# A decoder trunk on one core: the fourth weight sum of the gate/up strips formed by an adding transfer

## The chip, the core and the metric

The kernel runs on one core of a Trainium2 chip. The core has a matrix engine (TensorE, PE in the profile; PEld is its weight load), VectorE (DVE), ScalarE (ACT), GpSimd (POOL) and SyncE (SP), and 16 DMA engines that move data between the chip's main memory and the core's SBUF. The engines run side by side, each in the order of its own instructions, and wait for each other by semaphores. The metric is device time in microseconds of one execution, lower is better. Times of before are one profiled execution and three timed runs.

## The reference, cut to what matters

Two residual layers over 256 tokens of width 2048, all in float32. Each layer has a mixer, a cross attention into 256 memory tokens, and a SwiGLU feed-forward part:

```python
D_FF = -(-8 * D_MODEL // (3 * 256)) * 256     # 5632

def swiglu(h, w_gate, w_up, w_down):
    return (jax.nn.silu(h @ w_gate) * (h @ w_up)) @ w_down

for layer in range(DEPTH):                    # 2
    x = x + rmsnorm(mix, g[1])                # stick-breaking + pooling, or gated linear attention
    x = x + rmsnorm(memory_cross_attention(...), g[3])
    h = rmsnorm(x, g[4])
    x = x + rmsnorm(swiglu(h, ffn_w_gate[layer], ffn_w_up[layer], ffn_w_down[layer]), g[5])
```

The change touches `h @ w_gate` and `h @ w_up` alone: 256 x 2048 times 2048 x 5632, twice per layer.

## The kernel before

**Precision by splitting.** A float32 weight block w is split into a rounded part `w_hi`, written by ScalarE (`hi`, L542), and the rest `w_lo = w - w_hi`, written by VectorE (`lo`, L1017). The activations are split the same way. One product is then three matmuls: hi by hi, lo by hi, hi by lo.

**Strips and chunks.** Weights come in chunks of 128 x 2048 floats (1 MB, 8 KB on each of 128 partitions). SyncE loads them into five slots `wide0` to `wide4`, in turn (`load`, L330). ScalarE and VectorE split each chunk into one of four slots of `w_hi` and `w_lo`. A strip is 512 columns of each of two matrices (here gate and up) and takes eight chunks, n to n+7.

**Seven products in place of eight.** In most strips the first four chunks are treated as a 2 x 2 block matrix of weights b11, b12, b22, b21 (`B11, B12, B22, B21 = 0, 1, 2, 3` in order of loading), and the product is formed with seven block products in place of eight, from sums of weight blocks and sums of token blocks (`s_hi`, `s_lo`). So such a strip splits eleven chunks (`SUMMED = 11`), c to c+10: c = b11; c+1 = b11 + b12 (in `w_sum`); c+2 = the third sum (in b11's slot); c+3 = b21 as loaded; c+4 = the second sum (in b12's slot); c+5 = b22; c+6 = the fourth sum (in b21's slot); c+7 to c+10 = the last four chunks, n+4 to n+7, as they are. VectorE forms the four sums (`add`, L1021): three in `lead`, and the fourth at the head of `rest11`:

```python
dve.wait_ge(add_done, 4 * g + 3)
add(b21, b11, b21)
```

**What sets the order.** Each engine's program is written out by hand. On VectorE a strip is: split of c, three sums, splits of c+1 and c+2, the elementwise work of the strip before (`gather`: L1085 and L1522), split of c+3, the fourth sum, splits of c+4 to c+10. On ScalarE the copies of c to c+10 in the same order, with some moves between PSUM banks between them (L592 behind c+3; L600 behind c+4; L605 and L606 behind c+5, L614 behind c+7), of which TensorE waits for L614 ahead of product c+6. On TensorE one product per chunk c to c+6 (12 matmuls each; each waits for that chunk's `w_lo`), two per chunk c+7 to c+10, eight transposes behind c+3. A copy of chunk j waits until product j-4 is done (`w_used`), since there are four slots.

**When a slot is loaded again.** `slot_free` lists, load by load, the count that SyncE waits for: b11's slot is free when the fourth sum is done (it is its last reader), b12's when c+4 is split, b22's when c+5 is, b21's when c+6 is, and the last four when c+7 to c+10 are. With five slots, b11's slot takes the strip's sixth chunk, n+5, which is c+8. SyncE issues strictly in order.

**Where.** Per layer the gate/up stage has 11 strips, the first with eight plain products and ten with block sums, 20 in all. In other stages 15 more strips have block sums. In the gate/up stage GpSimd has nothing to do but to spill `xres` to memory ahead of it, to load a row of gains, and to reload `xres` once the tenth strip's product c+5 is done (`reload_x`, L434). GpSimd's transfers have a queue of their own.

Of the kernel before, what the change touches and what calls it, by code (L numbers as in the profile page):

```python
# [19 lines left out]
WIDE = 5  # L20
# [1 line left out]
SUMMED = 11  # L22
B11, B12, B22, B21 = 0, 1, 2, 3

Strip = namedtuple("Strip", "c n g a u")


def build(nc, x, mem, norms, mem_norm, even_w_in, pool_w, pool_scale, even_w_out, odd_w_in, gate_w,
# [14 lines left out]


    plan = {}
    at = {"c": 0, "n": 0, "g": 0, "a": 0, "u": 0, "r": 0, "rf": 0}
    slot_free = []
    STRIPS = FF // NB

    def stage(name, seven=(), rounds=0, rows=0, taken=True):  # L50

        pl = plan[name] = dict(at, strips=[])
        for summed in seven:
            st = Strip(at["c"], at["n"], at["g"] if summed else None, at["a"], at["u"])
            pl["strips"].append(st)
            for k in range(8):
                if summed and k == B11:  # L60
                    slot_free.append((1, 4 * st.g + 4))
                else:
                    chunk = {B12: 4, B22: 5, B21: 6}.get(k, k + 3) if summed else k
                    slot_free.append((0, 2 * (st.c + chunk + 1)))
            at["c"] += SUMMED if summed else 8
            at["n"] += 8
            at["g"] += 1 if summed else 0
            at["a"] += 2
            at["u"] += 1
        for k in range(rows):  # L70
            slot_free.append((0, 2 * (at["c"] + k + 1)))
        at["c"] += rows
        at["n"] += rows
        at["a"] += 1 if rows else 0
        at["u"] += 1 if rows else 0
        at["r"] += (rounds if taken else 0) + (1 if rows else 0)
        at["rf"] += rounds
# [6 lines left out]
    for l in range(LAYERS):  # L84
        stage(f"pre_mix{l}", rounds=2)
        if l == 0:
            stage("sb_qk", (False, True), rounds=2)
            stage("sb_z", rounds=1)
            stage("sb_vu", (True, True))
            stage("sb_sum", rounds=1)  # L90
            stage("sb_pv", rounds=1)
            stage("pool_mean", rounds=1)
            stage("pool_map", rounds=1)
        else:
            stage("gla_qk", (False, True), rounds=2)
            stage("gla_a", rounds=1)
            stage("gla_at", rounds=1)
            stage("gla_g", rounds=1)
            stage("gla_v", (False, True))
            stage("gla_s", rounds=1)  # L100
            stage("gla_r", (True, False))
            stage("gla_o", rounds=GH // 2)
            stage("gla_t", rounds=2)
        stage(f"mix_out{l}", (False, False))
        stage(f"pre_x{l}", rounds=2)
        stage(f"xq{l}", (False, True), rounds=2)
        stage(f"x_s{l}", rounds=1)
        stage(f"x_pt{l}", rounds=1)
        stage(f"x_pv{l}", rounds=2)
        stage(f"x_out{l}", (False, False))  # L110
        stage(f"pre_ff{l}", rounds=2)
        stage(f"gu{l}", (False,) + (True,) * (STRIPS - 1), rounds=STRIPS, taken=False)
        stage(f"down{l}", rows=FT)
    NORMS = ["mem_norm"] + [f"{n}{l}" for l in range(LAYERS) for n in ("pre_mix", "pre_x", "pre_ff")]
    POSTS = [f"{n}{l}" for l in range(LAYERS) for n in ("mix_out", "x_out", "down")]
# [6 lines left out]
    def sums_used(name, i):  # L122

        return strip_of(name, i).c + 6 + W_SLOTS
# [5 lines left out]
    with ExitStack() as ctx:  # L130
# [13 lines left out]
        def sem(name):  # L144
            return ctx.enter_context(nc.semaphore(name))
# [85 lines left out]

        wide_full = [sem(f"wide_full{i}") for i in range(WIDE)]
        add_done = sem("add_done")
        snap = sem("snap")
        prod_done = sem("prod_done")
        mid_taken = sem("mid_taken")
# [83 lines left out]
        @block.sync  # L320
        def _(sp):
            def load(n, src):

                if n >= WIDE:
                    summed, count = slot_free[n - WIDE]
                    sp.wait_ge(add_done if summed else lo_done, count)
                dst = wide[n % WIDE][:]
                if len(src.shape) == 3:
                    dst = dst.rearrange("p (k n) -> p k n", k=4)
                sp.dma_start(dst, src).then_inc(wide_full[n % WIDE], 16)  # L330

            def strip(st, w0, col0, w1, col1):

                order = [(q, s) for q in range(2) for s in range(4)]
                if st.g is not None:
                    order = [(0, 0), (1, 0), (1, 1), (0, 1), (0, 2), (0, 3), (1, 2), (1, 3)]
                for k, (q, s) in enumerate(order):
                    w, col = ((w0, col0), (w1, col1))[q]
                    load(st.n + k, cut(w, s)[:, :, col:col + NB])

            def strips(name, w, col0=0):
                for i, st in enumerate(plan[name]["strips"]):
                    col = col0 + i * 2 * NB
                    strip(st, w, col, w, col + NB)

            for l in range(LAYERS):
                strips(f"mk{l}", wk[l])
                strips(f"mv{l}", wv[l])
            for l in range(LAYERS):
                if l == 0:  # L350
                    strips("sb_qk", even_w_in)
                    strips("sb_vu", even_w_in, 2 * SBW)
                    strips("mix_out0", even_w_out)
                else:
                    strips("gla_qk", odd_w_in)
                    strips("gla_v", odd_w_in, 2 * GH * GK)
                    strips("gla_r", odd_w_in, 2 * GH * GK + GH * GV)
                    strips("mix_out1", odd_w_out)
                strips(f"xq{l}", wq[l])
                strips(f"x_out{l}", wo[l])  # L360
                for i, st in enumerate(plan[f"gu{l}"]["strips"]):
                    strip(st, w_gate[l], i * NB, w_up[l], i * NB)
                for k in range(FT):
                    load(plan[f"down{l}"]["n"] + k, w_down[l][k * P:(k + 1) * P, :])

            for m in range(MT):
                sp.wait_ge(x_done, 2 * len(POSTS) - 1 + m)
                sp.dma_start(out[m * P:(m + 1) * P, :], xres[:, m, :]).then_inc(y_out, 16)
            sp.wait_ge(y_out, 16 * MT)
# [3 lines left out]
        def _(pool):  # L373
            then = stepper(pool, pool_step)

            def load_gain(row):
                pool.dma_start(gain[:], row.partition_broadcast(P)).then_inc(gain_in, 16)
# [93 lines left out]
            for l in range(LAYERS):  # L471
# [37 lines left out]
                spill_x(2 * (3 * l + 2))  # L509
                pool.wait_ge(y_scaled, y_banks)  # L510
                load_gain(norms[l, 5])
                reload_x(2 * l + 1, sums_used(f"gu{l}", STRIPS - 1))
                if l < LAYERS - 1:
                    pool.wait_ge(work_full[7], plan[f"gu{l}"]["rf"] + STRIPS)
# [13 lines left out]
        def _(act):  # L528
# [30 lines left out]
            def lead(st, before_1=nothing, before_3=nothing):  # L559

                if st.g is None:
                    split(st, 0)
                    before_1()
                    split(st, 1)
                    split(st, 2)
                    before_3()
                    split(st, 3)
                    return
                hi(st.c, landed(st.n + B11))
                before_1()  # L570
                act.wait_ge(add_done, 4 * st.g + 1)
                hi(st.c + 1, w_sum[:, (st.c + 1) % W_SLOTS, :])
                act.wait_ge(add_done, 4 * st.g + 3)
                hi(st.c + 2, wide[(st.n + B11) % WIDE][:])
                before_3()
                hi(st.c + 3, landed(st.n + B21))
# [9 lines left out]
            def rest11(st, q_sb, p5_sb, reuse=(), before_5=nothing, before_9=nothing):  # L586
# [3 lines left out]
                act.wait_ge(w_used, c + 1 + W_SLOTS)  # L590
                act.wait_ge(bank_free[1], st.u + 1)
                nc.scalar.activation(ps[:, 1, :], ps[:, 0, :], ACT.Copy, scale=-1.0).then_inc(snap, 1)  # L592
                act.wait_ge(add_done, 4 * g + 2)
                hi(c + 4, wide[(st.n + B12) % WIDE][:])

                before_5()
# [7 lines left out]
                act.wait_ge(bank_free[3], st.u + 1)  # L604
                nc.scalar.activation(ps[:, 3, :], ps[:, 1, :], ACT.Copy).then_inc(snap, 1)  # L605
                nc.scalar.activation(q_sb, ps[:, 1, :], ACT.Copy).then_inc(snap, 1)  # L606
                act.wait_ge(add_done, 4 * g + 4)
                hi(c + 6, wide[(st.n + B21) % WIDE][:])
                split_wide = lambda j: hi(c + j, landed(st.n + j - 3))
                split_wide(7)  # L610
# [384 lines left out]
        def _(dve):  # L995
# [32 lines left out]
            def lead(st, before_1=nothing, before_3=nothing):  # L1028
# [15 lines left out]
                dve.wait_ge(w_used, c + 2)  # L1044
                add(w_sum[:, (c + 1) % W_SLOTS, :], b11, b12)
                loaded(st.n + B22)
                dve.wait_ge(add_done, 4 * g + 1)
                add(b12, b22, b12)
                dve.wait_ge(add_done, 4 * g + 2)
                add(b11, b12, b11)  # L1050
                lo(c + 1, w_sum[:, (c + 1) % W_SLOTS, :])
                lo(c + 2, b11)
# [11 lines left out]
            def rest11(st, before_5=nothing, before_7=nothing):  # L1064
                c, g = st.c, st.g
                b11, b12, b22, b21 = (src_of(st.n + k) for k in range(4))
                dve.wait_ge(add_done, 4 * g + 3)
                add(b21, b11, b21)
                lo(c + 4, b12)
                before_5()  # L1070
                lo(c + 5, b22)
                lo(c + 6, b21)
                before_7()
                for j in range(7, SUMMED):
                    lo(c + j, src_of(st.n + j - 3))
# [942 lines left out]
```

## Time and profile before

| | |
|---|---|
| median of 3 runs | 3009.91 us (2999.89, 3009.91, 3010.01) |
| the profiled execution | 2999.51 us, span of its instructions 2997.8 us |
| TensorE busy | 2886.9 us (96%) |
| VectorE busy | 2069.6 us (69%), of which 240.4 are 105 sums into `wide` |
| ScalarE busy | 1534.2 us (51%) |
| GpSimd busy | 99.6 us (3%) |
| moved by DMA | 583.44 MB, 195 GB/s over the span |
| mean granted TensorE clock | 0.985 |

The span is the time from the first to the last instruction of the execution that the profiler recorded. An engine is busy while one of its instructions runs; waiting and issuing transfers are not counted. A share over the whole span mixes stages with different limits, so what an edit in one stage is worth is read from that stage.

### The profile page before, as it was taken

Reading aid. Unit: us, or ns where it says so; the run is one execution under the profiler, and the core shown is the slowest. Engines: PE = TensorE matmul, PEld = TensorE weight load, DVE = VectorE, ACT = ScalarE, POOL = GpSimd, SP = SyncE. Lnnn points to the kernel's source line nnn. Section 1 sums busy time; section 2 is a strip of 40 time slices with the busy share of each in tenths; the row PEclk is TensorE's granted clock in tenths of the full one; section 3 lists DMA queues with packets and bytes.
Section 4 is the critical chain, followed back from the end, with each engine's and each line's share of the span. In section 5 each row is a group of like instructions: output and inputs, shape, how many; then the busy total and the mean of one; then the engine's idle time right before and its main releaser. Section 6 shows DMA issues by size and latency. Waiting matters only on the chain. (4 is left out here: it accounts for less than half of the span.)

```text
span 2997.8 us, 31678 instructions
## 1 busy us (share of the span) xinstructions
PE 2886.9 (96%) x13082; PEld 2389.9 (80%) x13082; DVE 2069.6 (69%) x1359; ACT 1534.2 (51%) x1363; POOL 99.6 (3%) x112
## 2 busy tenths in 40 slices
PE   7999999999999999999998999999999999999998
PEld 5888788778777888887887877777787788887887
DVE  6888778448348888885555758546646888886454
ACT  4666556445345556664344545444534665565443
POOL 0000000010010000000002000001001000000000
PEclk9999999999999999999999989999999999999999
DMA  7665744644445556556554615653554655565552
GB/s 266 225 255 180 282 179 157 242 166 173 166 165 204 183 202 225 216 182 252 193 195 157 213 68 187 238 204 133 197 182 168 219 182 182 204 225 226 205 189 96
DMA packets 237984, 583.44 MB, mean 195 GB/s; under 512 B 8720, under 2 KB 8736, under 8 KB 222096
## 3 DMA queue, kind: packets, MB, share of 16 engines
q1 hardware_dynamic: 232608, 530.61, 49.7%
q0 software_dynamic: 4064, 38.21, 3.2%
q10 hardware_dynamic: 1168, 12.59, 1.0%
q8 instruction: 104, 1.70, 0.2%
q14 instruction: 40, 0.33, 0.0%
HBM read 564.60 MB, written 16.78 MB: 194 GB/s over the span
## 5 line engine op out<-in xcount | busy, mean ns | idle before, releaser
L1017 DVE TENSOR_TENSOR w_lo<-wide,w_hi 128x2048 fp32r<-128x2048 f32 x550 | 1250.4, 2289 | 540.2 <-ACT w_hi L542 538.4
L542 ACT ACTIVATE w_hi<-wide 128x2048 fp32r<-128x2048 f32 x550 | 1048.8, 1914 | 557.1 <-PE ps L1568 443.4
L1568 PE MATMUL ps<-w_hi,act_hi 128*128 128x512 f32 x3332 | 1222.4, 393 | 36.2 <-DVE act_lo L1159 22.2
L1568 PE MATMUL ps<-w_hi,act_lo 128*128 128x512 f32 x3332 | 1217.3, 391 | 0.0
L1568 PE MATMUL ps<-w_lo,act_hi 128*128 128x512 f32 x3332 | 1217.1, 391 | 0.0
L1568 PEld LDWEIGHTS ps<-w_hi,act_hi 128*128 128x128 f32 x3332 | 629.6, 189 | 172.3 <-issue 30.8
L1568 PEld LDWEIGHTS ps<-w_hi,act_lo 128*128 128x128 f32 x3332 | 629.3, 189 | 131.7
L1568 PEld LDWEIGHTS ps<-w_lo,act_hi 128*128 128x128 f32 x3332 | 630.0, 189 | 130.7 <-issue 0.2
L1021 DVE TENSOR_TENSOR wide<-wide,wide 128x2048 f32<-128x2048 f32 x105 | 240.4, 2290 | 5.0
L1568 PE MATMUL ps<-w_hi,s_hi_x 128*128 128x512 f32 x528 | 211.1, 400 | 14.5 <-DVE nat L1513 6.3
L1568 PE MATMUL ps<-w_hi,s_lo_x 128*128 128x512 f32 x528 | 207.9, 394 | 0.0
L1568 PE MATMUL ps<-w_lo,s_hi_x 128*128 128x512 f32 x528 | 207.7, 393 | 0.0
L975 ACT ACTIVATE act_hi<-mid 128x256 fp32r<-128x256 f32 x80 | 33.4, 418 | 240.6 <-PE ps L1568 240.6
L1568 PEld LDWEIGHTS ps<-w_hi,s_hi_x 128*128 128x128 f32 x528 | 100.5, 190 | 36.1 <-DVE nat L1513 7.1
L1568 PEld LDWEIGHTS ps<-w_hi,s_lo_x 128*128 128x128 f32 x528 | 100.5, 190 | 21.5
L1568 PEld LDWEIGHTS ps<-w_lo,s_hi_x 128*128 128x128 f32 x528 | 100.7, 191 | 20.3
L1538 DVE TENSOR_TENSOR act_lo<-mid,act_hi 128x256 fp32r<-128x256 f32 x88 | 36.9, 424 | 114.1 <-ACT act_hi L975 114.1
L542 ACT ACTIVATE w_hi<-w_sum 128x2048 fp32r<-128x2048 f32 x35 | 67.2, 1921 | 88.1 <-DVE w_sum L1021 58.2
L1021 DVE TENSOR_TENSOR w_sum<-wide,wide 128x2048 f32<-128x2048 f32 x35 | 80.1, 2290 | 29.2 <-PE ps L1568 29.2
L718 ACT ACTIVATE ps<-ps 128x512 f32<-128x512 f32 x48 | 27.9, 582 | 117.9 <-DVE y L1209 117.9
L1017 DVE TENSOR_TENSOR w_lo<-w_sum,w_hi 128x2048 fp32r<-128x2048 f32 x35 | 79.9, 2284 | 0.0
L1209 DVE TENSOR_TENSOR y<-ps,gain 128x512 f32<-128x512 f32 x48 | 31.9, 687 | 66.1 <-PE ps L1568 42.7
(212 smaller groups left out, 1393.8 us busy)
## 6 DMA issues: line engine op xcount, KB each, us to landing
wide<-in_ffn_w_gate SPq DMA_DIRECT2D x88, 1024.0 KB, 7.6
wide<-in_ffn_w_up SPq DMA_DIRECT2D x88, 1024.0 KB, 7.2
wide<-in_ffn_w_down SPq DMA_DIRECT2D x88, 1024.0 KB, 4.9
wide<-in_odd_w_in SPq DMA_DIRECT2D x48, 1024.0 KB, 5.3
wide<-in_xattn_wk SPq DMA_DIRECT2D x32, 1024.0 KB, 8.3
wide<-in_xattn_wv SPq DMA_DIRECT2D x32, 1024.0 KB, 6.8
wide<-in_even_w_in SPq DMA_DIRECT2D x32, 1024.0 KB, 7.1
wide<-in_xattn_wq SPq DMA_DIRECT2D x32, 1024.0 KB, 5.1
```

The costliest lines, as they stand in the source:

```text
L542: nc.scalar.activation(w_hi[:, c % W_SLOTS, :], src, ACT.Copy).then_inc(hi_done, 2)
L718: nc.scalar.activation(bank, bank, ACT.Square, accum_out=ssq_part[:, m, part:part + 1])\
L975: nc.scalar.activation(act_hi[:, s % 4, :], mid[:, s, :], ACT.Copy).then_inc(jit_hi, 1)
L1017: nc.vector.tensor_tensor(w_lo[:, c % W_SLOTS, :], src, w_hi[:, c % W_SLOTS, :].bitcast(F32), ALU.subtract).then_inc(lo_done, 2)
L1021: nc.vector.tensor_tensor(out, a, b, ALU.add).then_inc(add_done, 1)
L1209: nc.vector.tensor_tensor(y[:, m, cols], ps[:, b, :], gain[:, cols], ALU.mult).then_inc(y_scaled, 1)
L1538: nc.vector.tensor_tensor(act_lo[:, s % 4, :], mid[:, s, :], act_hi[:, s % 4, :].bitcast(F32), ALU.subtract).then_inc(jit_done, 1)
L1568: return nc.tensor.matmul(dst, lhs, rhs, start=start, stop=stop, skip_group_check=loose)
```

## The change

The fourth sum is no longer a VectorE instruction in the 20 gate/up strips. GpSimd issues a transfer in its place, whose source is b11's slot and whose destination is b21's slot, with an adding operation: what is in the destination is read, the source added, and the sum written back. The 15 strips of other stages keep the VectorE instruction. A strip now also carries `k`, its first count of `add_done` (three sums per strip with the transfer, four else), and `d`, its number among the transfers (None without one). GpSimd waits for the third sum and for the split of c+3, the last reader of the loaded b21. ScalarE's copy of c+6 waits for the transfer (`dma_sum`, 16 per transfer), and so does SyncE before it loads into b11's slot.

```diff
-                    slot_free.append((1, 4 * st.g + 4))
+                    slot_free.append((2, 16 * (st.d + 1)) if by_dma else (1, st.k + 4))
...
+            at["k"] += (3 if by_dma else 4) if summed else 0
+            at["d"] += 1 if summed and by_dma else 0
...
-        stage(f"gu{l}", (False,) + (True,) * (STRIPS - 1), rounds=STRIPS, taken=False)
+        stage(f"gu{l}", (False,) + (True,) * (STRIPS - 1), rounds=STRIPS, taken=False, by_dma=True)
...
-                    sp.wait_ge(add_done if summed else lo_done, count)
+                    sp.wait_ge((lo_done, add_done, dma_sum)[summed], count)
...
                 pool.wait_ge(y_scaled, y_banks)
                 load_gain(norms[l, 5])
+                for i in range(1, STRIPS):
+                    st = strip_of(f"gu{l}", i)
+                    b11, b21 = (wide[(st.n + k) % WIDE] for k in (B11, B21))
+                    pool.wait_ge(add_done, st.k + 3)
+                    pool.wait_ge(lo_done, 2 * (st.c + 4))
+                    pool.dma_start(b21[:], b11[:], accum_op=ALU.add).then_inc(dma_sum, 16)
                 reload_x(2 * l + 1, sums_used(f"gu{l}", STRIPS - 1))
...
-                act.wait_ge(add_done, 4 * g + 4)
+                if st.d is None:
+                    act.wait_ge(add_done, st.k + 4)
+                else:
+                    act.wait_ge(dma_sum, 16 * (st.d + 1))
                 hi(c + 6, wide[(st.n + B21) % WIDE][:])
...
-                dve.wait_ge(add_done, 4 * g + 3)
-                add(b21, b11, b21)
+                if st.d is None:
+                    dve.wait_ge(add_done, st.k + 3)
+                    add(b21, b11, b21)
                 lo(c + 4, b12)
```

The other waits on `add_done` change from `4 * g` to `st.k` as their base, and nothing else.

On VectorE, before, from the split of c+3 to that of c+7 in the gate/up strip whose b21 lies in slot `wide0` (b11 in `wide2`):

```order
L1017 TENSOR_TENSOR w_lo_56<-wide0_49,w_hi_54 128x2048
L1021 TENSOR_TENSOR wide0_49<-wide2_51,wide0_49 128x2048
L1017 TENSOR_TENSOR w_lo_56<-wide3_52,w_hi_54 128x2048
L1017 TENSOR_TENSOR w_lo_56<-wide4_53,w_hi_54 128x2048
L1017 TENSOR_TENSOR w_lo_56<-wide0_49,w_hi_54 128x2048
L1017 TENSOR_TENSOR w_lo_56<-wide1_50,w_hi_54 128x2048
```

The second row goes, and the splits of c+4 and later follow the split of c+3 at once. On GpSimd, after, the transfers of the first layer stand between the row of gains and the reload of `xres`; each waits on two semaphores (here the last eight of the ten):

```order
L521 DMA wide1_50<-wide3_52 128x2048 [waits lo_done,add_done]
L521 DMA wide4_53<-wide1_50 128x2048 [waits lo_done,add_done]
L521 DMA wide2_51<-wide4_53 128x2048 [waits lo_done,add_done]
L521 DMA wide0_49<-wide2_51 128x2048 [waits lo_done,add_done]
L521 DMA wide3_52<-wide0_49 128x2048 [waits lo_done,add_done]
L521 DMA wide1_50<-wide3_52 128x2048 [waits lo_done,add_done]
L521 DMA wide4_53<-wide1_50 128x2048 [waits lo_done,add_done]
L521 DMA wide2_51<-wide4_53 128x2048 [waits lo_done,add_done]
L438 DMA xres_57<-x_scratch 128x4096 [waits w_used,x_kept]
```

Before, the reload of `xres` followed the row of gains directly; ten transfers now stand ahead of it.

## Rows read from the trace of the kernel before

**Rows 1.** The page: span, and busy time of each engine; weight loads (line group).
```profile
span 2997.8 us, 31678 instructions
PE 2886.9 (96%) x13082; PEld 2389.9 (80%) x13082; DVE 2069.6 (69%) x1359; ACT 1534.2 (51%) x1363; POOL 99.6 (3%) x112
...
L1568 PEld LDWEIGHTS ps<-w_hi,act_hi 128*128 128x128 f32 x3332 | 629.6, 189 | 172.3 <-issue 30.8
```

**Rows 2.** Busy time by stretch, both layers' ten gate/up strips with sums.
```profile
core 0: us, PE busy (x) PEld busy (x) DVE busy (x) ACT busy (x) POOL busy (x), PEclk, DMA share, GB/s
...
942.00:1359.00 417.00, 413.86 (x1866) 343.17 (x1865) 361.65 (x193) 254.44 (x193) 0.54 (x1) 1.00 0.56 203
...
2315.00:2732.00 417.00, 413.86 (x1859) 343.02 (x1858) 361.20 (x193) 254.31 (x192) 0.54 (x1) 1.00 0.55 202
```

**Rows 3.** Waits of TensorE, 908 to 1365 us: total, times, longest.
```profile
PE ps L1568 <- DVE nat L1513: 3.1, 1, 3.1
```

**Rows 4.** Timeline of VectorE: start us, us, instruction, [idle before <-releaser].
```profile
1192.03 2.29 DVE L1021 TENSOR_TENSOR w_sum<-wide,wide 128x2048 f32<-128x2048 f32 x1 [1.15 <-PE ps L1568]
...
1205.76 2.29 DVE L1017 TENSOR_TENSOR w_lo<-wide,w_hi 128x2048 fp32r<-128x2048 f32 x1
1207.97 2.28 DVE L1021 TENSOR_TENSOR wide<-wide,wide 128x2048 f32<-128x2048 f32 x1
1210.17 8.89 DVE L1017 TENSOR_TENSOR w_lo<-wide,w_hi 128x2048 fp32r<-128x2048 f32 x4
...
1230.28 2.29 DVE L1017 TENSOR_TENSOR w_lo<-wide,w_hi 128x2048 fp32r<-128x2048 f32 x1 [3.15 <-ACT w_hi L542]
1233.72 2.29 DVE L1021 TENSOR_TENSOR w_sum<-wide,wide 128x2048 f32<-128x2048 f32 x1 [1.15 <-PE ps L1568]
```

**Rows 5.** Timeline of ScalarE in the same strip.
```profile
1194.40 1.92 ACT L542 ACTIVATE w_hi<-w_sum 128x2048 fp32r<-128x2048 f32 x1 [1.88 <-DVE w_sum L1021]
...
1211.94 3.75 ACT L542 ACTIVATE w_hi<-wide 128x2048 fp32r<-128x2048 f32 x2
1217.30 0.58 ACT L614 ACTIVATE ps<-ps 128x512 f32<-128x512 f32 x1 [1.61 <-PE ps L1568]
...
1228.26 1.92 ACT L542 ACTIVATE w_hi<-wide 128x2048 fp32r<-128x2048 f32 x1 [3.52 <-PE ps L1568]
```

**Rows 6.** Timeline of TensorE where product c+6 of that strip starts.
```profile
1219.60 0.39 PE L1568 MATMUL ps<-w_hi,s_lo_x 128*128 128x512 f32 x1
1219.82 0.39 PE L1568 MATMUL ps<-w_hi,act_hi 128*128 128x512 f32 x1
```

**Rows 7.** Timelines of VectorE (578.94) and GpSimd (580.12, 580.71).
```profile
578.94 0.88 DVE L1292 SCALAR_TENSOR_TENSOR act_lo<-ps,vec,act_hi 128x256 fp32r<-128x256 f32 x2 [0.85 <-ACT act_hi L767]
...
580.12 0.56 POOL L377 DMA_DIRECT2D gain<-in_norms  x1 [46.95 <-DVE act_lo L1292]
580.71 0.54 POOL L498 DMA_DIRECT2D kx<-kv_scratch  x1
```

**Rows 8.** DMA engines, 1192.03 to 1233.72 us, 40 slices: busy tenths, rate.
```profile
DMA  3000000000000000003899999999999999999999
GB/s 147 26 0 0 0 0 0 0 0 0 0 0 0 0 0 0 0 0 75 291 409 411 381 399 230 377 377 366 409 405 399 389 385 389 387 387 381 393 389 346
```

**Rows 9.** Timeline of SyncE's queue; landing times of `wide`, 1192 to 1234 us.
```profile
1210.28 0.37 SPq L330 DMA_DIRECT2D wide<-in_ffn_w_gate  x1
...
DMA to landing us min/median/max: 4.9/7.7/8.2
```

**Rows 10.** GpSimd's DMA issues by stretch (1383 to 1390; 579 to 605): count, KB, landing.
```profile
pre_gain<-in_norms POOLq DMA_DIRECT2D x1, 1024.0 KB, 5.1
...
kx<-kv_scratch POOLq DMA_DIRECT2D x1, 2048.0 KB, 9.5
gain<-in_norms POOLq DMA_DIRECT2D x1, 1024.0 KB, 4.9
```

**Rows 11.** The trace's list of DMA issues: SyncE from SBUF.
```profile
out<-xres SPq DMA_DIRECT2D x2, 1024.0 KB, 3.9
```

**Rows 12.** The same list: GpSimd's 2 MB transfers beside other traffic.
```profile
xres<-x_scratch POOLq DMA_DIRECT2D x3, 2048.0 KB, 12.5
```

More of the change, by code:

```diff
@@ L23 @@
 B11, B12, B22, B21 = 0, 1, 2, 3
-Strip = namedtuple("Strip", "c n g a u")
+Strip = namedtuple("Strip", "c n g k d a u")
 def build(nc, x, mem, norms, mem_norm, even_w_in, pool_w, pool_scale, even_w_out, odd_w_in, gate_w,
@@ L45, in build, with stage @@
     plan = {}
-    at = {"c": 0, "n": 0, "g": 0, "a": 0, "u": 0, "r": 0, "rf": 0}
+    at = {"c": 0, "n": 0, "g": 0, "k": 0, "d": 0, "a": 0, "u": 0, "r": 0, "rf": 0}
     slot_free = []
     STRIPS = FF // NB
-    def stage(name, seven=(), rounds=0, rows=0, taken=True):
+    def stage(name, seven=(), rounds=0, rows=0, taken=True, by_dma=False):
         pl = plan[name] = dict(at, strips=[])
         for summed in seven:
-            st = Strip(at["c"], at["n"], at["g"] if summed else None, at["a"], at["u"])
+            st = Strip(at["c"], at["n"], at["g"] if summed else None, at["k"], at["d"] if by_dma else None,
+                       at["a"], at["u"])
             pl["strips"].append(st)
@@ L233, in build @@
         add_done = sem("add_done")
+        dma_sum = sem("dma_sum")
         snap = sem("snap")
@@ L570, in lead @@
                 before_1()
-                act.wait_ge(add_done, 4 * st.g + 1)
+                act.wait_ge(add_done, st.k + 1)
                 hi(st.c + 1, w_sum[:, (st.c + 1) % W_SLOTS, :])
-                act.wait_ge(add_done, 4 * st.g + 3)
+                act.wait_ge(add_done, st.k + 3)
                 hi(st.c + 2, wide[(st.n + B11) % WIDE][:])
@@ L592, in rest11 @@
                 nc.scalar.activation(ps[:, 1, :], ps[:, 0, :], ACT.Copy, scale=-1.0).then_inc(snap, 1)
-                act.wait_ge(add_done, 4 * g + 2)
+                act.wait_ge(add_done, st.k + 2)
                 hi(c + 4, wide[(st.n + B12) % WIDE][:])
@@ L1046, in lead @@
                 loaded(st.n + B22)
-                dve.wait_ge(add_done, 4 * g + 1)
+                dve.wait_ge(add_done, st.k + 1)
                 add(b12, b22, b12)
-                dve.wait_ge(add_done, 4 * g + 2)
+                dve.wait_ge(add_done, st.k + 2)
                 add(b11, b12, b11)
```

## The prediction

> **What bounds the kernel now.** I read the page's busy lines first. TensorE is busy 2886.9 of 2997.8 us and VectorE 2069.6 [rows 1], but these are averages over all stages, and the edit touches only the gate/up strips with block sums. So next I took the table of busy time by stretch for the two places where ten such strips run in each layer: in 417.00 us TensorE is busy 413.86, VectorE 361.65 and 361.20, at a granted clock of 1.00 [rows 2]. VectorE has 55 us to spare there and TensorE 3.1. The list of waits of TensorE puts all 3.1 us on one event, `nat` of VectorE's L1513, which happens in the first of the ten [rows 3]. So the strips are bound by the matmuls themselves. One strip lasts 1233.72 - 1192.03 = 41.69 us from one `w_sum` instruction to the next [rows 4].
>
> From here on I follow one strip, the one whose `w_sum` starts at 1192.03, and number its eleven split weight chunks c to c+10. The fourth sum, b21 = b11 + b21, becomes chunk c+6. On VectorE the last piece before it is the split of c+3 (1205.76, 2.29 us, so it ends at 1208.05), then the sum itself (1207.97, 2.28 us), then four splits in a row from 1210.17 [rows 4]. On ScalarE the copies of c+6 and c+7 are the pair that starts at 1211.94 [rows 5], so they start 1.7 us after the sum was ready. TensorE starts product c+6, the first matmul on `act_hi` after those on `s_hi_x`, at 1219.82, without a pause [rows 6].
>
> **What goes.** Ten strips in two layers lose one VectorE instruction each: 20 x 2.28 us = 45.6 us of VectorE time. None of it is on the path: what it leaves on VectorE is idle time, since the next `w_sum` waits for a matmul (the 1.15 us pause ahead of it [rows 4]) and TensorE has no gap to close. What it could free at most is the one gap of 3.1 us per layer [rows 3], 6.2 us in all, and even that gap is opened by work that stands ahead of the removed instruction. I count the removal at 0.
>
> **What comes: a transfer with a deadline.** GpSimd waits for the third sum and for the split of c+3, issues the transfer, and the copy of c+6 on ScalarE waits for its landing. Behind that copy ScalarE holds the copy of c+7 and the snapshot L614, without which TensorE may not start c+6 either. How late may the copy start? Backwards from 1219.82 [rows 6]: 0.19 for the weight load [rows 1] and 0.10 for a handoff, 2.29 for VectorE's split, 0.10 between ScalarE's end and VectorE's start (1228.26 + 1.92 = 1230.18 to 1230.28 [rows 4, 5]), 1.92 for the copy: 1219.82 - 4.60 = 1215.22. The snapshot path gives about the same: two copies from the same start, 3.75 us for the pair, and 0.58 [rows 5], are 4.33. From the end of the split of c+3, at 1208.05, this leaves 7.17 us.
>
> Of these, GpSimd's reaction takes 0.30: the VectorE piece at 578.94 lasts 0.88, to 579.82, and the transfer that waits for it is issued at 580.12 [rows 7]. ScalarE's reaction takes 0.08 (1192.03 + 2.29 to 1194.40 [rows 4, 5]). So the transfer may take 7.17 - 0.38 = 6.79 us from issue to landing before it costs anything; each microsecond above costs 20 us of the kernel, because the split of c+3 hangs on the former strip's matmuls and so moves with them.
>
> **How long does an adding transfer take?** The trace has none, so I bound it. In its time slot the DMA engines are idle: between about 1194 and 1210 the row shows zeros [rows 8], and SyncE's next load is issued only at 1210.28 [rows 9], which the edit moves behind the transfer. Quiet conditions therefore.
> - Low end: GpSimd's plain 1 MB transfer in such quiet landed after 5.1 us [rows 10], SyncE's from SBUF after 3.9 [rows 11]. Then it is hidden with 1.7 us or more to spare: cost 0.
> - Nearest for a transfer that reads both slots, 2 MB, and writes one: GpSimd issued 1 MB at 580.12 and 2 MB at 580.71; they landed 4.9 and 9.5 us later [rows 7, 10], at 585.02 and 590.21. The second 2 MB took 5.19 us, 2.6 per MB. So 5.1 + 2.6 = 7.7 us.
> - High end: GpSimd's 2 MB transfers beside other traffic took 12.5 us at the median [rows 12].
>
> I take 7.8: the 7.7, and 0.1 for the additional descriptors of a second source (my estimate, no row shows it). The excess over 6.79 is 1.0 us per strip, 20 us in all. At the high end it is 5.7 x 20 = 114 us.
>
> A rule of the Trainium skill speaks against the change here. The page "Collectives: The Full Stack", section "The bandwidth ceiling: the fold count and why AG ≠ RS ≠ AR", says that a reduce in the DMA engines reads two sources per chunk and so runs at about half of a copy, the add itself being free. No transfer in this trace adds, so only the changed kernel can show it; by the rule the data part doubles, as in my middle case. The Trainium skill's page "DMA: Bandwidth & Descriptors", section "Anatomy of one DMA — SWDGE (gpsimd) path", fits 2.0 us plus bytes over 436 GB/s, from which I estimate 4.4 us for 1 MB and 6.8 for 2 MB. The trace has 5.1 for the first, 0.7 more, so the rows decide; by the Trainium skill's figure the doubled transfer would just fit, and the time would be that of the first rival.
>
> **What is behind the transfer.** GpSimd has nothing else in these strips; its reload of `xres` stands behind the tenth and was issued after the strip's product c+5 anyway. SyncE is the queue that matters: the load of c+8 goes into b11's slot and now waits for the transfer, and all later loads behind it in order. In before it was issued at 1210.28, now at about 1216.2, 5.9 us later. It has to land by the copy of c+8: from the transfer's landing TensorE needs 4.6 us to start c+6, then 36 matmuls of 0.227 (1219.60 to 1219.82 [rows 6]), 8.2 us, and 4.6 of these are the copy, split and handoffs: 8.2 us are left for a load. SyncE's loads in this strip took 4.9 us at the least, 7.7 at the median and 8.2 at the most, sharing the DMA engines with each other [rows 9]. It fits. The burst itself needs 8 MB at about 390 GB/s, some 22 us (busy from 1211 to past 1233 [rows 8]), and now would end near 1240. The next strip's third block is the sixth of the eight, two loads (5.4 us) before the end, about 1234.5; VectorE wants it 2.4 us after the next `w_sum`, at 1237.1. Covered, with about 2 us.
>
> **Rivals.**
> - Hidden: the transfer lands within 6.8 us. Nothing changes but VectorE's busy time: 2999.5 us on the profile's scale, 3010 on the median's. For it: 5.1 and 3.9 for plain ones, the quiet slot, and an SBUF source. Against: it moves twice the reads. This is also the way to the other side, not slower; as a real gain it is worth at most the 6.2 us above, 0.2%.
> - A slow adder: the inline add or the two reads of one memory run at a third of the plain rate or below, 10 to 13 us. Excess 3.2 to 6.2, 64 to 124 us: 3075 to 3130. For it: no row shows what adding costs. Against: plain 2 MB alone need only 7.7.
> - Loads too late: the burst, 5.9 us later, is slower than reckoned by over 2 us (rows stored 2 KB at a time), so that the third block arrives after VectorE wants it. VectorE's chain to c+3 starts late, and with it the transfer: each microsecond costs 20 us again. With 1 us it is 20 us on top, 3050. Against: even the longest landing time of the strip, 8.2 us [rows 9], is no more than what is left.
> - GpSimd writes the descriptors slowly while VectorE works (it reads two SBUF slots at the time): issue took 0.54 to 0.60 us in all rows [rows 7], none longer, so I leave this inside the slow adder.
>
> **Numbers.** Forecast (7 to 9.5 us, 4 to 55 us more): 0.42. Hidden: 0.28. Slow adder: 0.23. Late loads: 0.05. A gain of any measurable size: 0.02. The sum is made on the profiled execution: 2999.5 us for a span of 2997.8, plus 20 = 3019.5. That execution is 10.4 us below the median of the three runs, 3009.91, which fall on two levels (2999.89; 3009.91, 3010.01). I forecast against the median: 3030 us. A range of its own for this case is 3005 to 3065; with the neighbours 2999 to 3110, which leaves out the top of the slow adder, about 0.12. 0.5% (15 us) is about what can be told from no change. A quarter of the forecast's case, below 0.75 us per strip, falls inside it: same 0.28 + 0.10 = 0.38; slower 0.60; faster 0.02.
>
> **What would show it.** Right: the page of after has 20 adding transfers of 1 MB that take 7 to 9.5 us; TensorE waits some 20 times for about 1 us at product c+6, on VectorE's split or on the snapshot; strips 42.7 us apart; VectorE busy 45.6 us less; the copy of c+6 waits for a DMA. The removal was free if no other gap of TensorE changes. Wrong: transfers under 6.8 us with strips still 41.7 apart (hidden); over 9.5 (slow adder); TensorE waiting at c+8 or VectorE waiting for loads ahead of its second sum (late loads).

## The result, and the profile after

The changed kernel takes 3020.98 us at the median of 7 runs (3017.68 to 3026.0), the one before 3005.94 us on the same occasion (7 runs, 2999.89 to 3010.03). The ratio is 1.005, 95% interval 1.0036 to 1.0064: 15 us slower, a small loss that is clear of noise. The profiled execution after took 3020.89 us, right at its median, while that of before (2999.51) lies at the low end of its runs. So of the 21.4 us between the two spans some 6 are the luck of the execution of before, and I count only what the strips show.

The page of after: span, busy time, and GpSimd's queue (packets, MB, share of 16 engines).

```profile
span 3019.2 us, 31698 instructions
...
PE 2897.7 (96%) x13082; PEld 2392.7 (79%) x13082; DVE 2028.2 (67%) x1339; ACT 1536.4 (51%) x1363; POOL 116.8 (4%) x132
...
q0 software_dynamic: 6944, 59.18, 6.6%
```

VectorE has 20 instructions and 41 us of busy time less than in [rows 1], GpSimd 20 instructions more. The strips got longer. The next rows are the ten `w_sum` instructions of each layer (count; min, median, max of one in ns; first and last start), of before and then of after:

```profile
L1021 DVE TENSOR_TENSOR w_sum<-wide,wide x10: 2284/2292/2294, 942.9 to 1317.1; 128x2048 f32<-128x2048 f32 x10
...
L1021 DVE TENSOR_TENSOR w_sum<-wide,wide x10: 2285/2292/2293, 2315.3 to 2691.1; 128x2048 f32<-128x2048 f32 x10
```

```profile
L1034 DVE TENSOR_TENSOR w_sum<-wide,wide x10: 2284/2288/2295, 946.0 to 1331.2; 128x2048 f32<-128x2048 f32 x10
...
L1034 DVE TENSOR_TENSOR w_sum<-wide,wide x10: 2284/2289/2293, 2333.1 to 2712.2; 128x2048 f32<-128x2048 f32 x10
```

Nine strips took 374.2 and 375.8 us before, and 385.2 and 379.1 after: 11.0 and 3.3 more, 14.3 in all, close to the 15.0 between the medians.

**One ordinary strip, 2458.67 to 2501.01.** VectorE's timeline of after (start, us; idle before, releaser). It answers to [rows 4].

```profile
2416.64 2.29 DVE L1034 TENSOR_TENSOR w_sum<-wide,wide 128x2048 f32<-128x2048 f32 x1
...
2458.67 2.29 DVE L1034 TENSOR_TENSOR w_sum<-wide,wide 128x2048 f32<-128x2048 f32 x1 [0.78 <-PE ps L1582]
...
2472.40 4.57 DVE L1030 TENSOR_TENSOR w_lo<-wide,w_hi 128x2048 fp32r<-128x2048 f32 x2
2477.39 2.29 DVE L1030 TENSOR_TENSOR w_lo<-wide,w_hi 128x2048 fp32r<-128x2048 f32 x1 [0.42 <-ACT w_hi L552]
2484.25 4.49 DVE L1030 TENSOR_TENSOR w_lo<-wide,w_hi 128x2048 fp32r<-128x2048 f32 x2 [4.57 <-ACT w_hi L552]
...
2498.80 2.29 DVE L1030 TENSOR_TENSOR w_lo<-wide,w_hi 128x2048 fp32r<-128x2048 f32 x1 [0.42 <-ACT w_hi L552]
2501.01 2.28 DVE L1034 TENSOR_TENSOR w_sum<-wide,wide 128x2048 f32<-128x2048 f32 x1
```

The splits of c+3 and c+4 now run as a pair, and before c+6 VectorE stands idle for 4.57 us: the 2.28 us that were removed have become waiting. The same strip on GpSimd, ScalarE (the copy of c+6 is the first of the pair at 2482.23; L627 is the snapshot that was L614) and TensorE (the start of product c+6), which answer to [rows 5, 6]:

```profile
2475.23 0.84 POOL L521 DMA_DIRECT2D wide<-wide  x1 [41.19 <-DVE w_lo L1030]
```

```profile
2482.23 3.73 ACT L552 ACTIVATE w_hi<-wide 128x2048 fp32r<-128x2048 f32 x2 [3.53 <-issue]
2485.86 0.59 ACT L627 ACTIVATE ps<-ps 128x512 f32<-128x512 f32 x1
```

```profile
2486.27 0.39 PE L1582 MATMUL ps<-w_hi,s_lo_x 128*128 128x512 f32 x1
2486.69 0.47 PE L1582 MATMUL ps<-w_hi,act_hi 128*128 128x512 f32 x1
```

Counted from `w_sum`, the transfer is issued at 16.56, the copy of c+6 starts at 23.56 (19.91 before), and product c+6 at 28.02 (27.79 before). TensorE's two matmuls are 0.42 us apart where 0.23 is the pace, so it waits 0.2 us. The list of waits leaves out so short a one, but twenty strips add them up.

The transfers themselves (issue time min, median, max in ns; landing):

```profile
L521 POOL DMA_DIRECT2D wide<-wide x20: 842/854/897, 961.4 to 2728.8; - x20
...
DMA to landing us min/median/max: 6.9/6.9/9.2
```

**Two more things cost.** First, w_sum starts are 42.03 us apart and then 42.34: the strip ends late in every second case. In the rows of VectorE the split ahead of `w_sum` at 2501.01 runs straight into it, where [rows 4] has a pause of 1.15 us. That split waited for ScalarE, and ScalarE for the load of the next strip's first block b11 (first row). In the second layer, 2315 to 2745 us, it waited for loads 16 times (total, times, longest); in the kernel before it waited for none in these strips:

```profile
2496.78 1.92 ACT L552 ACTIVATE w_hi<-wide 128x2048 fp32r<-128x2048 f32 x1 [0.79 <-DMA wide<-in_ffn_w_gate]
```

```profile
ACT w_hi L552 <- DMA wide<-in_ffn_w_up: 9.3, 7, 2.2
ACT w_hi L552 <- DMA wide<-in_ffn_w_gate: 7.4, 9, 1.1
```

Second, one transfer took 9.2 us. TensorE's list of waits (900 to 1390 us) and its timeline there:

```profile
PE ps L1582 <- DVE w_lo L1030: 5.7, 5, 3.0
```

```profile
1230.35 0.47 PE L1582 MATMUL ps<-w_hi,act_hi 128*128 128x512 f32 x1 [2.98 <-DVE w_lo L1030]
```

In that stretch, 1216 to 1227 us, an instruction fetch of 16 KB (q8) lay among the transfer's packets (q0). The traces of after, of the kernel with one wait and of the one that adds b21 to itself have two such transfers each: the six landed after 7.6 to 9.2 us, all others of after and of one wait after 6.9 to 7.0. That the fetch is what delays them is read from this coincidence; no run takes it away. The table by stretch shows the granted clock (third column from the end) falling after the wait, from 1.00 to 0.59 in the next 4 us, towards the lower of the two levels, 1.2 GHz:

```profile
q0 software_dynamic: 144, 1.05, 47.5%
q1 hardware_dynamic: 8, 0.02, 0.9%
q8 instruction: 1, 0.02, 0.6%
...
wide<-wide POOLq DMA_DIRECT2D x1, 1024.0 KB, 9.2
```

```profile
1226.00:1230.00 4.00, 1.38 (x7) 0.80 (x5) 2.08 (x1) 4.00 (x3) 0.00 (x0) 1.00 0.72 230
1230.00:1234.00 4.00, 3.65 (x9) 2.89 (x10) 3.04 (x3) 2.74 (x3) 0.00 (x0) 0.59 1.05 399
1234.00:1240.00 6.00, 6.00 (x28) 4.95 (x27) 5.15 (x3) 3.90 (x3) 0.00 (x0) 0.99 1.05 387
```

That strip lasted 45.85 us (`w_sum` at 1200.10 and 1245.95), 4 us above the 41.7 of before, and is over a quarter of the loss in this execution. The others were not traced, so whether each has such a strip stays open.

### The profile page after: what moved, and what is told of

It is laid out like the page before. It is cut to its first block and busy times, and to the rows that moved or that the text cites. A ratio compares the mean times of both kernels' runs of the same rounds, so it can differ in the third digit from the quotient of the medians.

```text
span 3019.2 us, 31698 instructions
## 1 busy us (share of the span) xinstructions
PE 2897.7 (96%) x13082; PEld 2392.7 (79%) x13082; DVE 2028.2 (67%) x1339; ACT 1536.4 (51%) x1363; POOL 116.8 (4%) x132
## 5 line engine op out<-in xcount | busy, mean ns | idle before, releaser
L1582 PE MATMUL ps<-w_hi,act_hi 128*128 128x512 f32 x3332 | 1224.5, 393 | 45.2 <-DVE act_lo L1173 22.7
L1034 DVE TENSOR_TENSOR wide<-wide,wide 128x2048 f32<-128x2048 f32 x85 | 194.7, 2291 | 5.0
L1582 PEld LDWEIGHTS ps<-w_hi,s_lo_x 128*128 128x128 f32 x528 | 100.4, 190 | 21.4
L1223 DVE TENSOR_TENSOR y<-ps,gain 128x512 f32<-128x512 f32 x48 | 31.9, 687 | 66.0 <-PE ps L1582 42.7
```

The costliest lines, as they stand in the source:

```text
L1034: nc.vector.tensor_tensor(out, a, b, ALU.add).then_inc(add_done, 1)
L1223: nc.vector.tensor_tensor(y[:, m, cols], ps[:, b, :], gain[:, cols], ALU.mult).then_inc(y_scaled, 1)
L1582: return nc.tensor.matmul(dst, lhs, rhs, start=start, stop=stop, skip_group_check=loose)
```

## The experiments

Three theories were at stake. A: the strip pays what the sum lands too late for product c+6. B: it pays because the loads behind the transfer are late. C: the relief of VectorE is worth something and hides part of the price. The copy of c+6 is counted from `w_sum`, which in the kernels with late loads is itself late in some strips. The kernels without a sum, with the plain copy, with half each and with the earlier split shared one set of runs of before; the loads held to c+5 and to c+6 and the two halves a second; the other three a third.

| kernel | ratio to before (95% interval) | landing, us | copy of c+6 after w_sum |
|---|---|---|---|
| after | 1.0050 (1.0036 to 1.0064) | 6.9 | 23.6 |
| no sum at all | 0.9999 (0.999 to 1.0008) | - | 19.9 |
| plain copy | 0.9999 (0.999 to 1.0008) | 4.5 | 21.1 |
| half each | 0.9999 (0.999 to 1.0008) | 4.5 | 21.2 |
| split of c+3 earlier | 1.0006 (0.9998 to 1.0015) | 6.9 | 22.7 |
| load held to c+5 (22.7) | 0.9998 (0.9989 to 1.0007) | - | 19.9 |
| load held to 23.7 | 1.0000 (0.9991 to 1.0009) | - | 19.9, in every second strip 19.1 |
| load held to c+6 (24.8) | 1.0080 (1.0067 to 1.0094) | - | 18.8 |
| two half transfers | 1.0028 (1.0017 to 1.0039) | 4.6, first half | 21.2, first half |
| adding b21 to itself | 1.0065 (1.0052 to 1.0078) | 7.3 | 24.0 |
| one wait on GpSimd | 1.0037 (1.0024 to 1.0049) | 6.9 | 23.3 |

**What the removal is worth.** From the kernel before (the condition put in words; b11's slot is then free after the split of c+3):

```diff
-                dve.wait_ge(add_done, 4 * g + 3)
-                add(b21, b11, b21)
+                if (not a gate/up strip):
+                    dve.wait_ge(add_done, 4 * g + 3)
+                    add(b21, b11, b21)
+                else:
+                    dve.sem_inc(add_done, 1)
```

> This kernel leaves the fourth weight sum out of the 20 gate/up strips (chunk c+6 is b21 alone) and puts nothing in its place; b11's slot is free after the split of c+3. It measures what the removal alone is worth. Theory A (the matmuls bound the strips and the removed VectorE instruction was covered): the time is that of before, within 0.2%, strips 41.7 us apart, VectorE busy 45 us less. Theory C (relief of VectorE is worth something and hides part of the transfer's cost): 3 to 6 us faster than before, the gap of 3.1 us in each layer's first strip goes.

VectorE is busy 2030.4 us, the time is that of before within 0.1%, and the wait of 3.1 us in the first strip is still there. The relief hides nothing that these runs can tell (3 us at most): theory C falls, and the 15 us are the transfer's price.

**Is it the adding?** From the changed kernel:

```diff
-                    pool.dma_start(b21[:], b11[:], accum_op=ALU.add).then_inc(dma_sum, 16)
+                    pool.dma_start(b21[:], b11[:]).then_inc(dma_sum, 16)
```

> This kernel leaves the addition out: the same 20 transfers from b11's slot to b21's, of the same 1 MB, but plain copies. Theory A (an adding transfer costs about 644 ns per 8 KB packet and engine against 309 for a plain one, and the strip pays what lands after the deadline): issue takes 0.55 us in place of 0.85, landing after 4.0 to 5.1 us, no wait of TensorE at product c+6, time as before within 0.2%. Theory B (the strip pays because the loads behind the transfer are late): the load of c+8 is still issued 3 us later than before, so strips stay above 41.7 us by 0.1 to 0.4, 3 to 8 us in all.

Nothing is left of the loss. The transfers of this kernel:

```profile
L521 POOL DMA_DIRECT2D wide<-wide x20: 537/538/540, 959.8 to 2712.3; - x20
...
DMA to landing us min/median/max: 4.3/4.5/4.8
```

So adding costs 0.31 us at the issue and 2.1 us more until the landing. That is 2.4 us from issue to landing, but this kernel's later loads start earlier too, so it alone does not tell theory A from B. Per packet: in a window of 7.10 us around one transfer (128 data packets of 8 KB on 16 engines) queue q0 is busy 73.0% in after, 0.730 x 7.10 x 16 / 128 = 0.65 us a packet, and 38.8% with plain copies, 0.34 us:

```profile
q0 software_dynamic: 144, 1.05, 73.0%
```

```profile
q0 software_dynamic: 144, 1.05, 38.8%
```

The Trainium skill's page "Collectives: The Full Stack" (section "The bandwidth ceiling: the fold count and why AG ≠ RS ≠ AR") says that a reduce in the DMA engines reads two sources and so runs at about half of a copy's rate. The rate agrees: 0.65 to 0.34 is a factor of 1.9. No run here shows that the second read is the reason.

**Half of it by each.** From the changed kernel, the transfer adds the left half and VectorE the right (ScalarE and SyncE then wait for both halves, which is left out here):

```diff
-                    pool.dma_start(b21[:], b11[:], accum_op=ALU.add).then_inc(dma_sum, 16)
+                    pool.dma_start(b21[:, :HALF], b11[:, :HALF], accum_op=ALU.add).then_inc(dma_sum, 16)
...
+                else:
+                    dve.wait_ge(add_done, st.k + 3)
+                    dve.wait_ge(lo_done, 2 * (c + 4))
+                    nc.vector.tensor_tensor(b21[:, HALF:], b11[:, HALF:], b21[:, HALF:], ALU.add)
+                        .then_inc(half_sum, 1)
```

> The transfer adds only the left half of the columns (512 KB) and VectorE the right half, after the split of c+3 (about 1.2 us). Theory A: landing after about 4.4 us (1.4 to the first packet, 8 packets of 4 KB at about 325 ns, 0.4 at the end), 2.5 us earlier than the full one, so no wait at c+6 and the time of before within 0.2%. Theory B: the load of c+8 is issued 2.7 us later than before; 1 to 5 us remain.

As theory A says: with the landing 2.4 us earlier the loss is gone, although c+8 is loaded 2.9 us later than in before.

**Only the start earlier.** From the changed kernel, in VectorE's program:

```diff
                     right_banks(gu[i], (q_sb[:], p5_sb[:]))
+                    between()        # the split of c+3
```

> As after, but VectorE splits c+3 between the two parts of the elementwise work of the strip before (behind L1099, ahead of L1536), which should end that split 0.8 us earlier; it can't be much more, since ScalarE copies c+3 only at that time. Theory A: the transfer lands 0.8 us earlier against product c+6, whose wait of 0.2 to 0.9 us goes in most strips; left are only transfers that another packet delays: 10 us of the 15 come back. Theory B: the burst of loads starts 0.8 us earlier as well, and part of the alternation 42.0/42.5 stays.

Splitting c+3 0.85 us earlier was enough for nearly all: 1.0006. The landing is 6.9 as in after, and the strips are 41.7 us apart again, with the pause before every second `w_sum` gone as in after:

```profile
2444.31 2.29 DVE L1034 TENSOR_TENSOR w_sum<-wide,wide 128x2048 f32<-128x2048 f32 x1 [0.82 <-PE ps L1586]
...
2486.04 2.29 DVE L1034 TENSOR_TENSOR w_sum<-wide,wide 128x2048 f32<-128x2048 f32 x1
...
2527.73 2.29 DVE L1034 TENSOR_TENSOR w_sum<-wide,wide 128x2048 f32<-128x2048 f32 x1 [1.15 <-PE ps L1586]
```

**Late loads without the transfer.** From the kernel before, three kernels, each with one later moment at which SyncE may load into b11's slot in the gate/up strips:

```diff
-                    slot_free.append((1, 4 * st.g + 4))        # fourth sum, 18.2 us after w_sum
+                    slot_free.append((0, 2 * (st.c + 5 + 1)))  # c+5 split, 22.7
+                    slot_free.append((2, 2 * (st.c + 8)))      # c+7 copied by ScalarE, 23.7
+                    slot_free.append((0, 2 * (st.c + 6 + 1)))  # c+6 split, 24.8
```

> As before, but in the gate/up stage SyncE may load into b11's slot only once c+5 is split, about 22.7 us after w_sum (before 18.2, after 23.5). Theory B: between before and the kernel that waits for c+6, 0 to 8 us. Theory A: time of before within 0.2%. If the waits by loads start only past some hour, this run shows whether the change was past it.

> As before, with VectorE's sum, but in the gate/up stage SyncE may load into b11's slot only once c+6 is split, about 24.9 us after the strip's w_sum in place of 18.2 (after has 23.5). It has the late loads without the transfer. Theory B (late loads cost by themselves): strips of 42.0 to 42.8 us, ScalarE waits for landings, w_sum starts without its pause of 1.15 us, 6 to 20 us in all. Theory A (only the late landing of the sum costs): strips 41.7 us, time of before within 0.2%.

> As before, with VectorE's sum, but in the gate/up stage SyncE may load into b11's slot only when ScalarE has copied c+7, 23.7 us after w_sum: the hour of after (23.5), without its transfer. Theory A (the late landing of the sum is the cause): no lengthening, strips 41.7 us. Theory B (the late loads are a cause of their own): the block b11 of the next strip lands after 37.3 us in every second strip, its copy and split push w_sum back, and those strips last 42.0 to 42.5 us: 2 to 6 us in all. The kernel that held the load until 22.7 us cost nothing and the one until 24.8 us 24 us, so the edge lies between.

At 22.7 and 23.7 us nothing is lost, at 24.8 us 24 us are, more than the 6 to 20 expected. Theory B as a cause of its own falls for after, whose moment was 23.5. But the timeline of VectorE with the load held to 23.7 shows what lateness does:

```profile
1070.04 2.29 DVE L1023 TENSOR_TENSOR w_sum<-wide,wide 128x2048 f32<-128x2048 f32 x1 [0.26 <-PE ps L1570]
...
1112.60 2.28 DVE L1023 TENSOR_TENSOR w_sum<-wide,wide 128x2048 f32<-128x2048 f32 x1
...
1153.46 2.29 DVE L1023 TENSOR_TENSOR w_sum<-wide,wide 128x2048 f32<-128x2048 f32 x1 [0.36 <-PE ps L1570]
```

The intervals are 42.56 and 40.86 us. Every second `w_sum` comes 0.9 us late because of a load, and the next is on time again: the slack of VectorE swallows it. With the full transfer in the strip there is no slack between `w_sum` and product c+6, so the same lateness moves the transfer and is paid; the kernel with one wait, below, shows it.

**The transfer without late loads.** From the changed kernel (SyncE's list of semaphores has `w_used` in place of `dma_sum`):

```diff
-                    slot_free.append((2, 16 * (st.d + 1)) if by_dma else (1, st.k + 4))
+                    slot_free.append((2, st.c + 4 + W_SLOTS) if by_dma else (1, st.k + 4))   # w_used
...
-                    pool.dma_start(b21[:], b11[:], accum_op=ALU.add).then_inc(dma_sum, 16)
+                    pool.dma_start(b21[:], b21[:], accum_op=ALU.add).then_inc(dma_sum, 16)
```

> This kernel computes another sum: the transfer adds b21's slot to itself, so b11's slot is not its source, and SyncE may load it again when product c+3 is done, 21.3 us after w_sum in place of 23.5. It has the transfer's landing without the late loads; the first load overlaps the last microsecond of the transfer. Theory A: landing after 6.9 to 7.3 us, TensorE waits 0.2 to 0.5 us at every c+6, strips a uniform 42.0 to 42.3, 6 to 11 us in all over before. Theory B: strips 41.7 but for a few.

Theory A's picture in kind, a late landing and uniform strips, but dearer than expected: 0.65%, about 20 us, where 6 to 11 were reckoned. The strips outside two disturbed ones are uniform and `w_sum` keeps its pause, so late loads play no part:

```profile
2416.45 2.29 DVE L1034 TENSOR_TENSOR w_sum<-wide,wide 128x2048 f32<-128x2048 f32 x1 [1.14 <-PE ps L1582]
...
2458.89 2.29 DVE L1034 TENSOR_TENSOR w_sum<-wide,wide 128x2048 f32<-128x2048 f32 x1 [1.15 <-PE ps L1582]
```

42.44 us are 0.73 over the 41.71 of before. The landing is 7.3 us: the load that was let in 2 us earlier shares the engines with the transfer's end (SyncE's queue q1 is busy 13.6% of the 8 us from the issue) and takes back 0.4 us. It is the load and not the changed source: in the first strip, where no load meets the transfer's end, it lands after 7.0 us, as in after. So 0.4 us of landing against 6.9 raised the strip's excess from 0.3 to 0.7: beyond the deadline it is one for one.

**GpSimd's reaction.** From the changed kernel:

```diff
-                    pool.wait_ge(add_done, st.k + 3)
                     pool.wait_ge(lo_done, 2 * (st.c + 4))
```

> As after, but GpSimd waits for the split of c+3 alone (the third sum is done before it anyway) and not for two semaphores. If the second wait is what makes GpSimd issue 0.54 us after the split of c+3 ended (0.30 was reckoned), the issue comes 0.2 us earlier, the copy of c+6 starts at 23.35 in place of 23.57 after w_sum, and about half of the 15 us comes back; if GpSimd's reaction doesn't depend on it, the time is that of after, 0.5% over before.

The second wait is what made GpSimd slow. Its timelines: the split of c+3 is the first of the pair, 2466.46 + 2.28 = 2468.74, and the issue follows 0.30 us later, where after has 0.55 (2472.40 + 2.28 to 2475.23).

```profile
2466.46 4.56 DVE L1029 TENSOR_TENSOR w_lo<-wide,w_hi 128x2048 fp32r<-128x2048 f32 x2
```

```profile
2469.04 0.84 POOL L520 DMA_DIRECT2D wide<-wide  x1 [40.92 <-DVE w_lo L1029]
```

The ratio falls from 1.0050 to 1.0037, a quarter to a third of the loss where half was reckoned, but the two intervals overlap, and in the trace two transfers were disturbed (8.4 and 9.2 us). The undisturbed strips tell more: from the second to the tenth `w_sum` of the second layer one strip lasts 41.99 us on average here, 42.25 in after and 41.71 in before. So half of the excess of such strips is gone. What is left lies in every second strip. TensorE at product c+6, of a strip whose `w_sum` was on time (2452.72) and of the next, whose `w_sum` was late (2494.93):

```profile
2480.51 0.46 PE L1581 MATMUL ps<-w_hi,act_hi 128*128 128x512 f32 x1
...
2522.72 0.47 PE L1581 MATMUL ps<-w_hi,act_hi 128*128 128x512 f32 x1 [0.22 <-DVE w_lo L1029]
```

Both start 27.79 us after their `w_sum`. The first has no pause ahead of it (the matmul before starts at 2480.29), so at 23.3 us the transfer is just in time; in the second the late `w_sum` is paid in full.

**Two halves.** From the changed kernel, two transfers of 512 KB, and copy and split of c+6 by halves (of which only the transfers are shown):

```diff
+                    for h in range(2):
+                        part = slice(h * HALF, (h + 1) * HALF)
+                        pool.dma_start(b21[:, part], b11[:, part], accum_op=ALU.add).then_inc(half_in[h], 16)
```

> As after, but the sum comes in two adding transfers of 512 KB on the same queue, and ScalarE's copy and VectorE's split of c+6 are done by halves, the first as soon as the first transfer landed. Theory A: the first half lands about 4.5 us after its issue, the second about 7.3, but only one half of copy and split (2.3 us in place of 4.3) follow it, so that c+6 is ready some 1.5 us earlier: no wait at c+6 in undisturbed strips, 8 to 12 of the 15 us come back. Theory B: the load of c+8 is issued no earlier (it waits for the second half), and what the loads cost stays, 3 to 8 us.

About 8 of 15 us are left, where theory A gave 3 to 7. The split of c+6's first half ends at 23.5 us after `w_sum`, but the second transfer lands no earlier than the one of after (c+8's load is issued at 23.8), and the `w_sum` starts swing as with late loads, only that here it is paid. How much belongs to which was not taken apart.

No version is faster than the kernel before; the best ones equal it.

## Why the prediction was right, and where it was not

I forecast 20 us on top, 0.7%, and 3030 us; measured are 15 us, 0.5%, and 3020.98 us. Of the 9 us between the two times 4 are before's, whose median was 3009.91 in three runs and 3005.94 in seven. The place and the mechanism held, a transfer that lands after its deadline. That the sum came so near is in part luck: the landing explains only some 6 of the 20 us, and late loads and disturbed transfers brought the rest. My own signs were half met: 18 of the 20 transfers took 6.9 to 7.0 us and not 7 to 9.5, and the strips are 42.0 to 42.8 us apart, not 42.7, but for one of 41.1 and the one of 45.85.

- **The removal counts 0.** Right: without any fourth sum the ratio is 0.9999.
- **The deadline.** Right within 0.15 us. I had the copy's latest start at 1215.22 - 1192.03 = 23.19 us after `w_sum`. In after it starts at 23.56 and product c+6 is 0.23 late, so the latest start is about 23.33; the kernel with one wait starts there and pays only in strips with a late `w_sum`. That it is a deadline, with nothing to pay ahead of it and one for one behind, the series of copies at 21.2, 22.7, 23.3, 23.6 and 24.0 us shows: 0, 0.06, 0.37, 0.50 and 0.65%, or, by the mean undisturbed strip, 41.71, 41.71, 41.99, 42.25 and 42.44 us (the late loads are in the third and fourth).
- **GpSimd's reaction, 0.30 us.** Wrong by 0.24: that row was of a transfer with one wait, and the change has two. The run with one wait showed it.
- **The landing, 7.8 us.** The term that was mis-sized: 6.9. The doubling of the data part was right (0.34 to 0.65 us a packet), but the plain base that I added it to was too long. The 5.1 us of [rows 10] are a load from memory; from SBUF to SBUF a plain 1 MB lands in 4.5, and the 3.9 of [rows 11] had pointed there. The surcharge of 0.1 us, put down to descriptors, was 0.3 at the issue. The excess of an undisturbed strip that starts on time thus was 0.3 us in place of 1.0, and 20 of them make 6 us. The 6.8 us that the prediction set beside its sum were nearly right; its sum would then have called the transfer hidden, and the longer reaction of GpSimd alone would have made that wrong.
- **Loads too late (5%).** This I valued wrongly. I reckoned the third block as the critical one, 2 us ahead; it is the first, b11, whose copy and split stand ahead of `w_sum`. It arrives too late in every second strip, and adds 0.3 to 0.5 us there, some 4 us in all. By itself it is harmless, as the load held to 23.7 us shows; it costs because the transfer has used up the slack. The rival was not another cause but an addition to the forecast.
- **What I had not on the list.** A transfer with an instruction fetch among its packets landed after 9.2 us; it brought a 3 us wait of TensorE, and some of its clock. 4 us of the loss came from that strip in the profiled execution.
- **Hidden (28%)** was nearer than 1.0 us of excess made it look: 0.85 us on the path or half of the data were enough, the 0.25 us of the second wait were not.

The sum by measured terms, for the 14.3 us in the strips: 0.3 us in each for the landing make 6, the late `w_sum` of every second strip 4, the disturbed strip 4 beyond an ordinary one, and the other disturbed transfer (landing 7.6 us) 1. Together these are 15; the strip in which each layer begins scatters by 1 to 2 us, so the terms can't be told more finely.

## What to carry to other kernels

An engine's spare instruction moved to a transfer saves nothing where another engine sets the pace, but it brings a deadline: work out from the consumer's side how late the result may land, and compare it with issue, landing and reactions to a tenth of a microsecond, for beyond it each strip pays one for one. An adding transfer took about twice a plain one's time per packet here (0.65 against 0.34 us). A transfer that keeps a buffer busy also delays the next load into it, which may be harmless alone and costly when the slack is used twice; starting it 0.85 us earlier, or giving it half the data, made it free here.

## What was not expected of the hardware

- GpSimd issues an adding transfer in 0.85 us and a plain one of the same shape in 0.54.
- GpSimd's transfer with two semaphores to wait for was issued 0.54 us after the later one's producer ended, with one 0.30.
- 512 KB adding and 1 MB plain landed equally, after 4.5 us.
- The loads swing from strip to strip: every second `w_sum` comes late, also without any transfer (load held to 23.7 us). Why every second one was not settled.
- After a wait of 3.0 us TensorE's granted clock was 0.59 over the next 4 us; after one of 2.7 us in the kernel with one wait it stayed at 1.00.
